# Expert outputs added up in DRAM by the scatter, in place of rows summed in the tail

## What is computed

```python
gates = route(h)                                   # (512, 64), 8 entries of each row are not zero
g = jnp.einsum('sd,edf->sef', hs, w_gate)
u = jnp.einsum('sd,edf->sef', hs, w_up)
act = jax.nn.silu(g) * u * gs[:, :, None]
routed = jnp.einsum('sef,efd->sd', act, w_down)
shared = (jax.nn.silu(h @ ws_gate) * (h @ ws_up)) @ ws_down
y = routed + shared
x = x + ga2 * rmsnorm(y, g_post_ffn)
```

## Time and profile before

| | |
|---|---|
| median of three runs | 1127.2 us |
| the profiled execution, its own time | 1130.07 us |
| its span, first to last instruction | 1128.3 us |
| TensorE (PE) busy | 1055.3 us, 94% |
| VectorE (DVE) busy | 749.7 us, 66% |
| ScalarE (ACT) busy | 569.6 us, 50% |
| GpSimd (POOL) busy | 514.7 us, 46% |
| mean granted TensorE clock | 0.969 |
| moved by DMA | 318.66 MB, 282 GB/s on average |
| of it on GpSimd's queue (q0) | 45.40 MB |

### The profile page before, as it was taken

One profiled execution on the slowest core, in us unless ns is written; L12 is line 12 of the kernel. 1 busy time (PEld: TensorE's weight loads), 2 busy tenths in 40 slices (PEclk: granted clock), 3 DMA queues, 4 the chain that ended last, 5 costly groups with the idle time before them and its releaser, 6 DMA issues.

```text
span 1128.3 us, 14598 instructions
## 1 busy us (share of the span) xinstructions
PE 1055.3 (94%) x4532; PEld 726.3 (64%) x4532; DVE 749.7 (66%) x1274; ACT 569.6 (50%) x606; POOL 514.7 (46%) x222
## 2 busy tenths in 40 slices
PE   4899997889789999999999999999999999999966
PEld 0687785548554666776677666766676667667622
DVE  1659764743764867777777777777777777677347
ACT  5334235742341655665566556665566556556311
POOL 1233213630330566656665666556655665564100
PEclk9799997989898999999999999999999999999989
DMA  9666742111242699999999999999998889898287
GB/s 343 226 241 259 280 153 65 65 43 62 104 195 88 231 350 351 365 352 374 368 383 358 362 360 353 359 363 366 372 358 334 340 343 346 330 351 349 85 362 307
DMA packets 67911, 318.66 MB, mean 282 GB/s; under 512 B 17136, under 2 KB 17648, under 8 KB 40368
## 3 DMA queue, kind: packets, MB, share of 16 engines
q1 hardware_dynamic: 43152, 269.51, 62.2%
q0 software_dynamic: 22624, 45.40, 11.1%
q10 hardware_dynamic: 2112, 3.45, 0.9%
HBM read 317.25 MB, written 39.85 MB: 316 GB/s over the span
## 4 chain that ended last, share of the span: by engine, by line
PE 81%; DVE 9%; DMA 6%; issue 2%; ACT 2%; SPq 0%; ACTq 0%; DVEq 0%; POOLq 0%; POOL 0%
PE ps L1269 20%; PE ps L1250 11%; PE ps L1252 11%; PE ps L1251 11%; PE ps L963 8%; PE ps L1033 7%; DMA yall<-y_rows 3%; PE ps L1183 3%; PE ps L1158 2%; PE ps L979 1%; PE ps L1089 1%; PE ps L1115 1%; PE ps L1203 1%; DVE acc L1402 1%; DMA ada<-in_w_ada_dram 1%
## 5 line engine op out<-in xcount | busy, mean ns | idle before, releaser
L606 POOL DMA_INDIRECT hg<-h_rows,idxg x70 | 344.1, 4916 | 147.5 <-DVE idxg L1709 145.2
L1715 DVE TENSOR_TENSOR wlo<-raw,whi 128x2048 fp32r<-128x2048 f32 x134 | 300.5, 2282 | 0.0
L841 ACT ACTIVATE whi<-raw 128x2048 fp32r<-128x2048 f32 x136 | 261.3, 1922 | 0.1
L1269 PE MATMUL ps<-rawd,actt 128*128 128x512 f32 x544 | 244.5, 592 | 1.4 <-ACT actt L877 1.4
L1250 PE MATMUL ps<-whi,hthi 128*128 128x512 f32 x544 | 225.3, 414 | 0.0
L1252 PE MATMUL ps<-whi,htlo 128*128 128x512 f32 x544 | 213.0, 392 | 0.0
L1251 PE MATMUL ps<-wlo,hthi 128*128 128x512 f32 x544 | 212.8, 391 | 0.0
L1729 DVE TENSOR_TENSOR htlo<-ps,hthi 128x1024 fp32r<-128x1024 f32 x68 | 83.3, 1225 | 176.6 <-ACT hthi L873 176.6
L883 ACT ACTIVATE ysb<-ps 128x1024 f32<-128x1024 f32 x68 | 69.6, 1024 | 213.5 <-PE ps L1269 213.5
L1269 PEld LDWEIGHTS ps<-rawd,actt 128*128 128x128 f32 x544 | 102.8, 189 | 104.7 <-issue 97.8
L614 POOL DMA_INDIRECT y_rows<-ysb,idxs x68 | 73.3, 1077 | 169.4 <-ACT ysb L883 164.6
(11 more groups left out here) (254 smaller groups left out, 1303.2 us busy)
## 6 DMA issues: line engine op xcount, KB each, us to landing
raw<-in_w_gate_dram SPq DMA_DIRECT2D x68, 1024.0 KB, 8.0
raw<-in_w_up_dram SPq DMA_DIRECT2D x68, 1024.0 KB, 11.1
rawd<-in_w_down_dram SPq DMA_DIRECT2D x68, 1024.0 KB, 13.2
ada<-in_w_ada_dram SPq DMA_DIRECT2D x24, 1024.0 KB, 8.2
yall<-y_rows SPq DMA_DIRECT2D x8, 2048.0 KB, 22.9
wraw<-in_w_in_dram POOLq DMA_DIRECT2D x8, 1024.0 KB, 5.6
woraw<-in_w_out_dram SPq DMA_DIRECT2D x16, 256.0 KB, 2.8
xs<-in_x_dram SPq DMA_DIRECT2D x4, 512.0 KB, 5.7
```

The source lines that it names most:

```text
L606: gp.indirect_dma_start(out=hg[s][:, :, :].rearrange("p k q -> p (k q)"), out_offset=None, in_=h_rows, in_offset=bass.IndirectOffsetOnAxis ...
L841: A(whi[:, s, :, cols], raw[:, s, :, cols], ACT.Copy).then_inc(hi_ok, 1)
L1269: ins = mm(bank(4 + hf), actt[:, k, :], rawd[:, s, k, hf * 512:(hf + 1) * 512], start=(k == 0), stop=(k == KF - 1))
L1715: V.tensor_tensor(wlo[s][:, :, c0:c1], raw[:, s, :, c0:c1], whi[:, s, :, c0:c1].bitcast(F32), ALU.subtract).then_inc(lo_dve, 1)
```

## The change

`y_rows` is no longer one tensor with a row for each token and rank. There are two, one for each slot s, each with 512 rows, a row for each token. A scatter of slot s adds its rows to table s in DRAM (`compute_op=ALU.add`) where it wrote them before, and `idxs` is now the token, with indices over 511 skipped. As two scatters may name the same token, each one waits until the scatter before it on its table has landed.

Table 1 begins with zeros: SyncE writes them from `hg[1]`, which GpSimd clears, before the first gather into it. Table 0 begins with the shared expert's rows: ScalarE writes `ysh` to it, after its step for block 1, and the first scatter waits for that (`ysh_out`).

In the tail SyncE reads each table in four pieces of 512 KB, table 0 as soon as its own last scatter has landed. TensorE's part is gone. VectorE adds the two tables' rows for a tile and multiplies by `ga2` (`scaled`), and does that for the next tile ahead of the factor and the residual of this one.

```diff
-        y_rows = nc.dram_tensor("y_rows", [TOPK * T, D], F32, kind="Internal").ap()
+        y_rows = [nc.dram_tensor(f"y_rows{s}", [T, D], F32, kind="Internal").ap() for s in range(SLOTS)]
@@ SyncE, after the last of h2 and the first down weights
             load_down(0, 0)
 
+            sp.wait_ge(zero_ok, 1)
+            for t in range(TT):
+                sp.dma_start(y_rows[1][t * P:(t + 1) * P, :], hg[1][:, :, :].rearrange("p k q -> p (k q)"))\
+                  .then_inc(zero_out, 16)
@@ SyncE, tail
             for s in range(SLOTS):
                 sp.wait_ge(scattered[s], m * 16 + 16 * (E // 2))
-            for t in range(TT):
-                for g in range(2):
-                    sp.dma_start(yall[:, t, 4 * g:4 * g + 4], y_v[t][:, 4 * g:4 * g + 4]).then_inc(y_in[2 * t + g], 16)
+                for t in range(TT):
+                    sp.dma_start(ysum[:, s, t, :], y_rows[s][t * P:(t + 1) * P, :]).then_inc(y_in[TT * s + t], 16)
@@ GpSimd
             def scatter(i, s):
                 gp.wait_ge(y_ok, num(i, s) + 1)
                 gp.wait_ge(idxs_ok, num(i, s) + 1)
+                if isinstance(i, int) and i == 0:
+                    if s == 0:
+                        gp.wait_ge(ysh_out, 16 * TT)
+                else:
+                    gp.wait_ge(scattered[s], i * 16)
                 gp.sem_inc(scatter_go, 1)
-                gp.indirect_dma_start(out=y_rows, out_offset=bass.IndirectOffsetOnAxis(ap=idxs[s][:, 0:1], axis=0),
-                                      in_=ysb[s][:, :], in_offset=None,
-                                      bounds_check=last_routed, oob_is_err=False).then_inc(scattered[s], 16)
+                gp.indirect_dma_start(out=y_rows[s], out_offset=bass.IndirectOffsetOnAxis(ap=idxs[s][:, 0:1], axis=0),
+                                      in_=ysb[s][:, :], in_offset=None, bounds_check=last_row, oob_is_err=False,
+                                      compute_op=ALU.add).then_inc(scattered[s], 16)
...
             gather(0, 0)
+            gp.wait_ge(zero_out, 16 * TT)
             gather(0, 1)
@@ ScalarE
             step_act(0, 1, 1)
+            ac.wait_ge(sdn_ev, TT)
+            for t in range(TT):
+                ac.dma_start(y_rows[0][t * P:(t + 1) * P, :], ysh[t][:, :]).then_inc(ysh_out, 16)
             step_act(1, 0, 2)
@@ TensorE, tail
-            for t in range(TT):
-                part_sum(t)
@@ VectorE
             def rows_of(i, s):
...
-                V.tensor_copy(idxs[s][:, :], col(destr, num(i, s))).then_inc(idxs_ok, 1)
+                V.tensor_scalar(idxs[s][:, :], col(destr, num(i, s)), 3, None, ALU.logical_shift_right)\
+                 .then_inc(idxs_ok, 1)
@@ VectorE, tail
+            def scaled(t):
+                y = ysum[:, 0, t, :]
+                v.wait_ge(y_in[t], 16)
+                v.wait_ge(y_in[TT + t], 16)
+                V.tensor_tensor(y, y, ysum[:, 1, t, :], ALU.add).then_inc(ysum_ok, 1)
                 v.wait_ge(ysum_ok, t + 1)
-                then(V.tensor_tensor(yall[:, t, 0, :], y, ga2[:, :], ALU.mult))
+                then(V.tensor_tensor(ytmp[:, t, :], y, ga2[:, :], ALU.mult))
...
+            scaled(0)
+            for t in range(TT):
+                if t + 1 < TT:
+                    scaled(t + 1)
                 rows_done(t)
```

More of the change, by code:

```diff
@@ L80, in block_kernel @@
         wlo = [at("wlo0", [P, 2, 2048], F32R, 96 * KB), at("wlo1", [P, 2, 2048], F32R, 80 * KB)]
-        yall = at("yall", [P, TT, TOPK, D], F32, 0)
+        ysum = at("ysum", [P, 2, TT, D], F32, 0)
+        ytmp = at("ytmp", [P, TT, D], F32, 32 * KB)
         ada = [at(f"ada{s}", [P, 2, D], F32, (0, 8, 136, 112, 120, 128)[s] * KB) for s in range(ADA_SLOTS)]
@@ L336, in block_kernel @@
         destr_ok = sem("destr_ok")
-        y_in = [sem(f"y_in{t}_{g}") for t in range(TT) for g in range(2)]
-        ypart_mm = sem("ypart_mm")
+        ysh_out = sem("ysh_out")
+        zero_ok = sem("zero_ok")
+        zero_out = sem("zero_out")
+        y_in = [sem(f"y_in{s}_{t}") for s in range(SLOTS) for t in range(TT)]
+        ysum_ok = sem("ysum_ok")
         root_set = sem("root_set")
-        ysum_ok = sem("ysum_ok")
         out_ok = sem("out_ok")
@@ L350, in block_kernel @@
         wd_v = w_down.rearrange("e (p k) n -> e p (k n)", k=KF)
-        y_v = y_rows.rearrange("(t p r) n -> t p r n", r=TOPK, p=P)
         SC1, SH1, GA1, SC2, SH2, GA2 = 1, 0, 2, 4, 3, 5
@@ L379, in block_kernel @@
         GU_BANK = [6, 2]
-        Y_BANK = [0, 2, 6, 0]
-        Y_PE, Y_DVE = (0, 1, 2, 4), (5, 6, 7)
         OV = 2 * BANK
@@ L526, in then @@
                 gp.wait_ge(pool_step, step[0])
-            last_row, last_routed = gp.to_reg(T - 1), gp.to_reg(NO_ROW - 1)
+            last_row = gp.to_reg(T - 1)
             def pick(tile, op, fill, pattern, mult, base_=0):
@@ L625, in _ @@
             gp.memset(hg[0][:, :, :], 0.0)
-            then(gp.memset(hg[1][:, :, :], 0.0))
+            gp.memset(hg[1][:, :, :], 0.0).then_inc(zero_ok, 1)
+            gp.wait_ge(zero_ok, 1)
             for half in range(2):
@@ L953, in _ @@
                 ac.wait_ge(ysum_ok, t + 1)
-                A(junk[:, :], yall[:, t, 3, :], ACT.Square, accum_out=stat[:, ST_S, t:t + 1]).then_inc(sumsq, 1)
+                A(junk[:, :], ysum[:, 0, t, :], ACT.Square, accum_out=stat[:, ST_S, t:t + 1]).then_inc(sumsq, 1)
                 take_root(ST_S, t, t + 1)
@@ L1796, in rows_done @@
                     cols = slice(hf * 512, (hf + 1) * 512)
-                    V.scalar_tensor_tensor(out=xs[:, t, cols], in0=yall[:, t, 0, cols], scalar=rs[:, ST_S, t:t + 1],
+                    V.scalar_tensor_tensor(out=xs[:, t, cols], in0=ytmp[:, t, cols], scalar=rs[:, ST_S, t:t + 1],
                                            in1=xs[:, t, cols], op0=ALU.mult, op1=ALU.add).then_inc(out_ok, 1)
+            scaled(0)
             for t in range(TT):
-                add_rows(t)
+                if t + 1 < TT:
+                    scaled(t + 1)
                 rows_done(t)
```

## The result

The changed kernel is slower. Its median is **1154.9 us** (1151.4 to 1156.5, four runs), that of the kernel before on the same chip 1128.9 us; the ratio is 1.0227, with a 95% interval of 1.019 to 1.0263: slower for certain, while it stays open whether by more than 2%. The forecast was 1110 us, faster, with a range that ended at 1150. The profiled execution took 1153.7 us, within the other runs; its span of 1152.0 is 23.7 us longer than that of before.

The account below looks back on a forecast made before the run. TensorE was taken to set the pace, with the DMA engines right behind. From 1127.2 us, minus 26 (tail), plus 1 (ahead of the loop), plus 8 (loop) gave 1110 us; the range was 1100 to 1150.

Parts of the forecast that it names:

- What bounds the kernel: Expert loop: TensorE, busy for all 100 us of each 100 us stretch, sets the pace at 10.23 us per block.
- right behind it: Expert loop: DMA engines stand next after TensorE, with mean busy shares of 0.97, 0.95 and 0.91 in three stretches.
- The price of the accumulation: Loop scatters: adding costs one more copy, 0.72 us of all engines per block, within bounds of nothing and 1.44 us.
- Where it is over 1, the loop follows the DMA engines: First 43 blocks: busy share reaches 1.04 and 1.02, costing some 0.025 of 10.23 us each, 11 us; last 24 nothing.
- The 8 us: Loop: net loss forecast from the accumulation, 11 us in 43 blocks less 3 us taken up by slack.
- The slack: Loop: time before transfers are late, 1.1 us for up weights and 2.4 us for the gather; the scatter has room.
- the 3 us: Loop: part of the 11 us loss that the slack was said to take up once.
- The dear rival: Loop: accumulating scatter costs three copies, 1.44 us more; gather late first, or descriptors over 2.6 us; about 1152 us, chance 0.27.
- The hidden rival: Loop: accumulation is hidden, blocks keep 10.23 us and the time is 1102 us; chance 0.25.
- The tail: After the last scatter: less reading and VectorE as the bound save 26 us, ends 23 to 28.
- I cost them at nothing: Tail: table 0's 2 MB of reads come in during the last block's down projection and scatter; 4.9 us if uncovered.
- Ahead of the loop: Before the loop and block 1: zeros cost nothing, shared-row writes on ScalarE's queue 1 us, ends 0 and 4.

Follow-up runs that it names:

- the spread one: Changed kernel with the first 64 tokens of a block on the first two of every four partitions, same bytes and adds: median 1113.8 us, ratio 0.9839, loop 670.4 us.
- light loads: Changed kernel with loop weight refills of 128 KB instead of 1 MB, once with adding and once with plain scatters: both loops 670.4 us.
- the spread kernels: Changed kernel with its adds and permuted slots, such as first 64 tokens on the first two of every four partitions, or on 0 to 31 and 64 to 95: loops 670.4 us.

## Why the prediction was wrong

- **What bounds the kernel** held: TensorE sets the pace, and the DMA engines are what stands next. But "right behind it" was read off a mean of 16. The kernel before had the last of its engines 3 to 4 us behind the first eight in the loads of weights; no row of mine could show that, as a landing is the last count of sixteen.
- **The price of the accumulation**, one more copy, 0.72 us of all engines, was right: 0.75 in the changed kernel, 0.72 in the spread one. The Trainium skill, "Collectives: The Full Stack", section "The bandwidth ceiling: the fold count and why AG ≠ RS ≠ AR", speaks of two source reads in place of one, which was that value. Under load the trace agrees; beside light loads the addition is 1.27 us, 1.8 times that value.
- **The step that failed** is the next one: "Where it is over 1, the loop follows the DMA engines". It failed both ways. At a mean of 0.90 to 0.95 the changed kernel loses 44.6 us in its loop (37.5 in the first 42 periods, 7.1 in the last 24, where nothing was forecast); at 1.00 to 1.02 the spread kernels lose none. What held TensorE up was the last count of each load, that is the fullest engines: 12 to 17.5 us where it was 8.4 to 13.3. The 8 us were thus not a term of the wrong size but one from the wrong quantity. (Even as it stands the term is a little low: the shares it quotes, 1.04 and 1.02, are 0.03 over 1 and give 13 us, not 0.025 and 11.) A bound from the earlier trace rows would have warned: if all gathered and scattered rows went through half of the engines, these stood at 79.9 + 2 × 14.3 = 108% before, and the addition would come on them twice over. It is a warning and no threshold, since the kernel before lost nothing at that value, and with three quarters of the rows there it is 101%.
- **The slack** was measured well and used badly. The up weights had 1.1 us and were late first, as the numbers said; but I took the 3 us off once as a gift, where by the chain of waits the cycle over two blocks (load, high half, low half, next load) returns a lateness to its own start.
- **The dear rival** came close to the time, 1152, and was wrong in each reason: not three copies but two, not the gather first but the weights, and 1.59 us for the scatter's descriptors, not over 2.6. That it is near the measured 1155 us is luck. The hidden rival is right for the kernel with spread slots: loop 670.4 us.
- **The tail** gave 21.9 us, not 26 and outside the ends of 23 to 28. VectorE's part was right (21.0 us for 21.2), and so was the distance from the landing to the end (27.2 for about 27). The failing term is "I cost them at nothing": table 0's reads did hide behind the last block, but in front of its scatter, which took 4.5 us longer to land.
- **Ahead of the loop** it was 4.6 us, not 1, just over the upper end of 4. The writes fell into a stretch that I called not yet full and delayed the gather by more than it had to give. The zeros cost nothing that shows.

## What to carry to other kernels

A mean DMA share says nothing on the fullest engine: before loading the queues further, look at how far the counts of one transfer lie apart, and ask which partitions a partly filled tile leaves empty. Where rows are gathered or scattered by index, spread the valid ones over the partitions (here one changed pattern was worth 46 us of loop with accumulation, and 1 us without). Where a load's buffer is freed by work that waits for the load itself, look at the length of that whole cycle (here 22.8 us against 20.5) and not only at the slack of one load.

## What the runs showed of the hardware

- Partitions and engines: beside accumulating scatters with the first 64 rows of a block on partitions 0 to 63, or on the first four of every eight, the last count of a 1 MB load came at 11.9 and 11.5 us; with them on 0 to 31 and 64 to 95, or on the first two of every four, at 7.4 and 7.6.
- An accumulating scatter of some 65 rows of 4 KB (500 to 900) cost 0.72 to 0.75 us of all engines more than a plain one while the engines were full, 327 ns for the median packet where a plain one has 159, and 1.27 us at a mean share of 0.49, where it landed after 6.0 instead of 3.3 us. Its descriptors took GpSimd 1.59 us, a plain one's 1.01.
- The mean DMA share can stand at 1.01 at 373 GB/s, and at 1.01 at 403 GB/s, with TensorE never waiting in that stretch: it isn't a measure of how much more goes through.
- Near the end of a wait of 2.69 us TensorE's granted clock fell to the 1.2 GHz level for 6.8 us, and that period took 16.05 us for 10.23.
- An indirect DMA took GpSimd 1.0 us to issue by itself and 5.2 to 5.4 us where it started beside VectorE's subtraction of two SBUF tensors (a gather in nearly every block of the kernel before).
